# Scores of a gated recurrence: blocks of 32 tokens on column quarters of TensorE, two levels at a time

## The reference, cut to what matters

```
b = cumsum(g)                                     # g = log f
decay[t, s, c] = exp(b[t, c] - b[s, c])           # for s <= t, else 0
scores[t, s] = sum over c of q[t, c] decay[t, s, c] k[s, c]
o[t] = sum over s of scores[t, s] v[s]  +  (q[t] exp(b[t])) S
S_new = exp(b_last) S + sum over s of (k[s] exp(b_last - b[s])) v[s]
```

## Time and profile before

| | us |
|---|---|
| median of 3 runs | 2412.07 (2411.49 to 2412.95) |
| the profiled execution | 2411.33 |
| span of its trace | 2409.6 |
| PE busy | 2341.5 (97%) |
| PEld busy | 1945.4 (81%) |
| DVE busy | 1476.3 (61%) |
| ACT busy | 931.2 (39%) |
| POOL busy | 374.8 (16%) |

### The profile page before, as it was taken

How to read it: one execution, slowest core, us unless ns; L and a number is a source line. 1 busy time by engine, 2 the same in 40 slices (tenths; PEclk the granted TensorE clock), 3 DMA queues, 4 the chain that set the end, 5 groups by cost and what they waited for, 6 DMA issues and landing times. The chain is left out here.

```text
span 2409.6 us, 32379 instructions
## 1 busy us (share of the span) xinstructions
PE 2341.5 (97%) x11821; PEld 1945.4 (81%) x11821; DVE 1476.3 (61%) x2012; ACT 931.2 (39%) x1511; POOL 374.8 (16%) x498
## 2 busy tenths in 40 slices
PE   5999999999999999999999999999999999899998
PEld 4888887676788788888888888888888888688886
DVE  6766644765444766644556666666666667757655
ACT  3222322643433322233335544444444444553223
POOL 0111100000000111100033443333333333100000
PEclk8999999999999999999999999999999999999999
DMA  7766643221123667633311121111121111123231
GB/s 272 235 218 210 200 140 101 78 70 53 53 96 97 205 214 222 205 117 98 100 53 45 52 62 55 60 53 53 53 62 53 53 56 58 58 71 96 88 95 54
DMA packets 69430, 254.02 MB, mean 105 GB/s; under 512 B 7616, under 2 KB 7744, under 8 KB 69312
## 3 DMA queue, kind: packets, MB, share of 16 engines
q1 hardware_dynamic: 51312, 186.82, 24.3%
q0 software_dynamic: 18000, 65.56, 8.0%
HBM read 250.25 MB, written 2.10 MB: 105 GB/s over the span
## 5 line engine op out<-in xcount | busy, mean ns | idle before, releaser
L208 PE MATMUL ps<-hH,wh 128*128 128x512 f32 x1648 | 660.2, 401 | 5.8 <-issue 3.1
L204 DVE TENSOR_TENSOR wl<-raw,wh 128x1024 fp32r<-128x1024 f32 x331 | 410.8, 1242 | 389.4 <-ACT wh L199 384.2
L210 PE MATMUL ps<-hH,wl 128*128 128x512 f32 x1648 | 643.2, 390 | 0.0
L209 PE MATMUL ps<-hL,wh 128*128 128x512 f32 x1648 | 642.2, 390 | 0.0
L199 ACT ACTIVATE wh<-raw 128x1024 fp32r<-128x1024 f32 x331 | 348.0, 1052 | 247.7 <-PE ps L210 240.8
L208 PEld LDWEIGHTS ps<-hH,wh 128*128 128x128 f32 x1648 | 309.8, 188 | 72.8 <-issue 12.8
L210 PEld LDWEIGHTS ps<-hH,wl 128*128 128x128 f32 x1648 | 309.3, 188 | 66.2
L209 PEld LDWEIGHTS ps<-hL,wh 128*128 128x128 f32 x1648 | 310.0, 188 | 63.6 <-issue 3.8
L1889 POOL TENSOR_TENSOR XR<-XR,fp 128x512 f32<-128x512 f32 x112 | 143.1, 1278 | 580.2 <-ACT KQ L1573 580.2
L540 POOL DMA_DIRECT2D araw<-in_ada x120 | 63.8, 532 | 870.9 <-ACT rs L264 365.6
L208 PE MATMUL ps<-sH,wh 128*128 128x512 f32 x352 | 139.4, 396 | 0.0
(11 more groups left out here) (367 smaller groups left out, 3767.3 us busy)
## 6 DMA issues: line engine op xcount, KB each, us to landing
raw<-in_ws SPq DMA_DIRECT2D x331, 512.0 KB, 3.5
araw<-in_ada POOLq DMA_DIRECT2D x120, 512.0 KB, 4.9
praw<-in_ada SPq DMA_DIRECT2D x16, 512.0 KB, 10.7
xin<-in_x SPq DMA_DIRECT2D x1, 2048.0 KB, 9.7
out_x<-xout SPq DMA_DIRECT2D x1, 2048.0 KB, 6.4
cin<-in_ctx POOLq DMA_DIRECT2D x1, 1024.0 KB, 5.3
cst<-in_const SPq DMA_DIRECT2D x1, 512.0 KB, 3.6
mask<-in_mask POOLq DMA_DIRECT2D x1, 512.0 KB, 3.7
```

The costliest lines, as they stand in the source:

```text
L204: dve.tensor_tensor(wl[:, j, :], raw[:, j, :], wh[:, j, :].bitcast(F32), ALU.subtract).then_inc(lo_ready, 1)
L208: pe.matmul(o, a_hi, b_hi, start=start, stop=False, **kw)
L209: pe.matmul(o, a_hi, b_lo, start=False, stop=False, **kw)
L210: return pe.matmul(o, a_lo, b_hi, start=False, stop=stop, **kw)
```

## The change

Each 128x128 product of a set becomes four products of 32-wide weights (32 keys), each on its own column quarter of the array (`tile_position=(0, 32 * b)`), and with only those queries as moving columns which the set needs: the same block of 32 for sets 0 to 5, the sibling block of 32 for set 6, the other 64 for set 7. The order on PE becomes: values, sets 0 and 1, context product of f1, (w), sets 2 and 3, q, sets 4 and 5, z (or w3), sets 6 and 7, transposes. On DVE the operations are put in an order to match. ACT and POOL are unchanged.

```diff
             for c in range(4):
-                r = slice(c * P, (c + 1) * P)
-                last = pe.matmul(ps[:, 6 + j % 2, r], kt_[:, r], qt_[:, r], start=True, stop=True, skip_group_check=True)
+                for b in range(4):
+                    s0, n = c * P + 32 * b, 64 if j == NL else 32
+                    t0 = c * P + (64 * (1 - b // 2) if j == NL else 32 * (b ^ 1) if j == NL - 1 else 32 * b)
+                    last = pe.matmul(ps[32 * b:32 * b + 32, 6 + j % 2, t0:t0 + n], kt_[:, s0:s0 + 32], qt_[:, t0:t0 + n],
+                                     start=True, stop=True, skip_group_check=True, tile_position=(0, 32 * b))
             last.then_inc(h_sc, 1)
...
+            value_pe(pe, i)
             scores_hg(pe, i, 0)
-            value_pe(pe, i)
             scores_hg(pe, i, 1)
...
-            scores_hg(pe, i, 2)
             if OUT_FROM <= i and more:
...
                 last.then_inc(slot_done, 1)
+            scores_hg(pe, i, 2)
             scores_hg(pe, i, 3)
...
             scores_hg(pe, i, 4)
+            scores_hg(pe, i, 5)
             if "z" in a and more:
...
-                if part < 3:
-                    scores_hg(pe, i, 5 + part)
+            scores_hg(pe, i, 6)
+            scores_hg(pe, i, 7)
...
+            split("f1" if more else "w1")
             place(dve, i, 0)
-            split("f1" if more else "w1")
             level_dve(dve, i, 1)
...
             level_dve(dve, i, 2)
-            place(dve, i, 2)
-            outs(0, 2)
-            level_dve(dve, i, 3)
-            outs(2, 4)
+            outs(0, 4)
             if not more:
                 z_dve(dve, i)
+            place(dve, i, 2)
+            level_dve(dve, i, 3)
+            place(dve, i, 3)
             split("w" if more else "w2")
-            place(dve, i, 3)
             level_dve(dve, i, 4)
             if more:
                 split("q")
+                query_dve(dve, i + 1)
             place(dve, i, 4)
-            if more:
-                query_dve(dve, i + 1)
             level_dve(dve, i, 5)
```

## The result

| | before | after |
|---|---|---|
| median, us | 2412.51 (4 runs, beside the new kernel) | 2390.16 (4 runs, 2386.05 to 2391.24) |
| ratio, 95% interval | | 0.9902 [0.9888, 0.9916] |
| the profiled execution, us | 2411.33 | 2386.05 |
| span of its trace, us | 2409.6 | 2384.4 |

The kernel became 0.98% faster, by 22.4 us in the medians.

The account below looks back on a forecast made before the run. TensorE's own time was taken as the bound. Cheaper sets with mode changes -25.1 us, the stall -5.0, +1.5 back: -28.6 on 2411.33 gives 2382.7, median 2383.5 us (about -1.2%), range 2364 to 2446.

Parts of the forecast that it names:

- What bounds, and the cost of a set before: TensorE's own time, PE busy 97% of the span; a set of eight records costs 0.89 us, eight sets 7.12 a step.
- Quarters work beside each other: In the sets, products on different column quarters overlap; only the two records of one product follow each other; chance 0.53.
- the first rival: In the sets, quarters run in series, 28 ns load a record: 2438 us (2430 to 2446), slower; chance 0.33.
- 30 ns a product: In the sets, one move plus issue for each two-record product: 0.48 us a set, 0.91 for set 7.
- Changes of mode, 0.32 us a group: Around each group of sets on PE: 0.12 us into the mode, 0.20 out, 1.28 us a step for four groups.
- The stall ahead of the query product: PE's 0.54 us wait for DVE's output additions in steps 5 to 14 goes; -5 us in all.
- The levels' chain: Ahead of the transposes, slack 1.6 us plus 0.4; set gains beyond about 2 us a step lost, 3 in steps 5-13.
- The transposes' wait should stay under 0.3 us: Sign to check: PE's transposes waiting for the last level in steps 0 to 4; over 1 us would show the prediction wrong.
- Step 14, the chain "which stays": Uncovered levels behind set 4, 6.3 us, stay; only sets 0 to 3 and half the changes of mode count.
- "+1.5 back" for steps 14 and 15: Allowance of 1.5 us returned for the last two steps, whose sets lack cover (+2 us in step 15).
- The clock: Rival: short records with gaps lower PE's clock in each step, +25 to +50 us on top; chance 0.03.
- The break-even of 46 ns a product: In the sets, the cost from which the change loses: 46 ns a product, 23 a record.

Follow-up runs that it names:

- the order alone: The changed kernel's order on PE and DVE, with the 128x128 products of the kernel before; 2412.34 us, ratio 0.9999.
- both: Changed kernel with half of v ahead of the transposes, all of v before sets 6 and 7 in step 14, last step's w2 behind set 3; 2358.85 us.
- same_quarter: Changed kernel with its two inner loops exchanged, so four products in a row use the same column quarter; 2409.07 us, ratio 0.9985.
- halves: Changed kernel with each 128x128 product in two 64-wide halves of the array instead of four quarters; 2390.66 us in a single execution.
- f1_behind: Changed kernel with DVE's split of the f1 slot put back behind place 0; 2401.68 us, ratio 0.9961.

## Why the prediction was right, and where its steps were not

The time was met within 0.3%, and the gain was 22.4 us where 29 were forecast (from the median of before). That it came so close is luck: two errors nearly cancelled, sets that are cheaper than forecast and waits that were not in the sum. Step by step:

- **What bounds, and the cost of a set before**: right. 0.89 us a set, confirmed by 1.79 us for two sets, sixteen records, in the order alone.
- **Quarters work beside each other, the first rival falls**: right. The records start 8.8 ns apart on average, far below the load of 28 ns that the rival wanted in series. Quarter by quarter, the same products cost 20.5 ns.
- **30 ns a product**: the term that was mis-sized. Measured 17 ns. The step that failed is "the next quarter's product starts when the second record of this one has started": a pair doesn't hold up the other quarters. Each quarter keeps its own pace of 32 ns a record, and 2 x 32 / 4 = 16 ns is what comes out. A set costs 0.28 us instead of 0.48; set 7 about 0.45 instead of 0.91. It lay just above the lower bound of 14 ns.
- **Changes of mode, 0.32 us a group**: right. Into it 0.09 (forecast 0.12), the whole group 0.89 - 0.55 = 0.34.
- **The stall ahead of the query product**: right for the order alone (0.6 us a step gone), half right in the changed kernel, where 0.24 of the 0.54 us stay. The prediction had "both sets 2 and 3 (0.32 + 0.96)" between w and q, "more than one addition of 0.7"; they take 0.57 us and a change of mode of 0.3, and that is too short, since the addition starts only when w's last product is out.
- **The levels' chain**: right in kind and counted short. Sets and changes went from 7.12 to about 3.7 us a step, 3.4 saved instead of 1.57. I had said that gains beyond some 2 us in steps 0 to 4 and 3 in steps 5 to 13 would be lost. What was left is 1.1 a step in steps 1 to 4, and 2.5 in steps 5 to 13 (2.8 less the 0.3 that the stall gives). The slack was read at DVE's last level alone, 1.6 us; POOL's operation, which the third group of transposes needs, had 0.8 us in the trace of before, and now it comes 0.5 us later still than DVE's. By this reading even the forecast's own 1.57 us went beyond the slack (no run shows that case). "The transposes' wait should stay under 0.3 us" was wrong: 0.8 to 1.5 for DVE and 0.5 for POOL in steps 0 to 4. By the prediction's own words (a wait of over 1 us) that should have broken it; the cheaper sets made up for it.
- **Step 14, the chain "which stays"**: right in kind. But what the earlier sets gave was lost too: 0.0 in all. The sets' stretch is 1.2 us shorter, what follows it 2.1 us longer at the lower clock.
- **"+1.5 back" for steps 14 and 15**: the term that was furthest off. By the prediction's sum the two steps together gain 2.1 us (2 x 1.57 + 0.5 - 1.5); measured, step 14 gains nothing and step 15 takes 6.5 us more than before (7.4 less set 0). Against the measured price of the sets 13.8 us were given back, 3.9 in step 14 and 9.9 in step 15. I counted the sets without cover in it and overlooked a chain over three engines: set 2 behind w2, merge 3, ACT's z, DVE's gating, place 2, set 4. In the trace of before, where set 2 stood ahead of w2, the gating waited 0.2 us; the order of the code on PE and ACT would have told it.
- **The clock**: its price as a rival (every step) did not come, but in the last two steps it did, at 0.90 over step 14 and 0.83 over step 15.
- **The break-even of 46 ns a product**: by the sum's own terms it is 44 to 45. Nothing hangs on it at 17 ns.

The account with the measured terms: 16 x -3.4 = -54.4 for the sets; -5.9 for the order in ten steps, as the order alone has it; given back 10.7 in steps 0 to 4 and 10.5 in steps 5 to 13, of which 2.2 are the stall that stays and the rest is the levels' chain; 3.9 in step 14; 9.9 in step 15. That makes -25.3, as in the traces. What was given back is worked out as the rest of each step, so that the sum can't test it; the waits of 15.0 us shown above and the 2.2 us of the stall are most of the 21.2 in steps 0 to 13. Of 60 us taken off PE's stream, 35 didn't arrive; `both` is 31 us faster than the changed kernel.

The rule of the Trainium skill on a floor of about 60 cycles for a matmul ("TensorEngine Tiling (Array Packing)", Instruction Overhead) is not borne out across quarters: 8.8 ns a record is a third of the 25 ns that it makes (an estimate, 60 cycles at 2.4 GHz). Within one quarter the measured 32 ns would allow it. The Trainium skill's other rule, that packed tiles start about 4 ns after each other ("TensorE: Matmul & The Clock Gate", Part 3), is near the 5 ns at a change of quarter in `same_quarter`.

The clock doesn't need short products to fall. The order alone has full ones and the same kind of wait in its last step, and behind it the rounded products start 0.43 us apart in place of 0.23, for some 6 us. Timeline of PE in its last step:

```profile
2048.73 1.13 PE L1344 MATMUL ps<-KQ 128*128 128x128 f32 x8 [3.88 <-DVE scT L1712]
2050.65 2.08 PE L1344 MATMUL ps<-KQ 128*128 128x128 f32 x8 [0.79 <-ACT KQ L1574]
...
2055.08 0.63 PE L208 MATMUL ps<-y0H,wh 128*128 128x512 f32 x1
...
2057.85 0.39 PE L208 MATMUL ps<-y0H,wh 128*128 128x512 f32 x1
```

Cheap sets do leave PE idler where nothing covers the chain of levels, and the clock went with that. The stretch of sets 4 to 7 in step 14, in the kernel before and in the changed one (columns as above):

```profile
2000.90:2008.20 7.30, 4.37 (x35) 3.79 (x34) 5.32 (x8) 3.08 (x7) 4.01 (x5) 1.00 0.24 73
1966.30:1973.50 7.20, 2.57 (x130) 2.10 (x129) 6.51 (x10) 3.03 (x7) 5.01 (x7) 0.69 0.42 145
```

The chain is as long, and PE is busy for 2.57 us of it instead of 4.37. Over the whole of step 14 the clock is 0.90 to 0.94 in all seven traces whose sets are cheap (0.28 us, 0.47 in `halves`) and whose stretch is uncovered. It is 1.00 in the traces of the kernel before, `order_only` and `same_quarter`, whose sets take 0.65 us and more, and in `both`, which covers the stretch. That is one trace of each kernel, and no run changes PE's idle time there and nothing else.

What stays open: the end of the last step was at half the clock in the changed kernel (9.26 us) and at the full one in `f1_behind` (6.43), with the same stream on PE; no run separates chance from cause there, nor in the executions that have no trace.

## What to carry to other kernels

If a product is used only in blocks on its diagonal, split the weights by column quarters, go round the quarters in the innermost loop, and count one quarter's pace divided by four, plus about a third of a microsecond for entering and leaving the mode. Before you count a gain on the bounding engine, follow every producer of the next thing it waits for, not the latest one on one engine, and place independent work in the gap that will open there. After moving work in a hand-written order, look at the first and last turns of the loop by themselves: there the cover is different, and one queue's order can close a chain over three engines.

## What the runs showed of the hardware

- Four column quarters really run at once in float32: 8.8 ns a record of 32 by 32 columns on average, 32 ns in one quarter alone; halves of 64 columns 29 ns on average.
- The issue of matmuls doesn't stand in the way down to 17 ns for a product of two records.
- Behind a wait of 1.3 us on PE the clock was at half for a few us in one step of `f1_behind` (1.6 us lost), and not in the next three steps with the same waits. Its executions, with the same instructions, spread over 10 us, the fastest at a mean clock of 0.989, the others at 0.985 and 0.986.
- With PE busy for 2.57 of 7.20 us in step 14 the clock was 0.69 there; with 4.37 of 7.30 it stayed at 1.00.
